# Filling the unused rows of the experts' results inside phase two instead of at the experts' start

## The chip, the cores and the metric

The kernel runs on one core of a Trainium2 chip. The metric is the device time of one execution in microseconds. Three executions of the kernel before took 2258.63, 2264.56 and 2267.71 us; the time that counts is their median, 2264.56 us.

## What is computed

One inference step of one decoder layer, in float32, for a prompt of 2048 tokens and 8 sample tokens with states of their own (D = 1024). What matters here:

```python
h = x + W_out[ concat(mLSTM heads, chunk MLP heads) ]( rmsnorm(x) )
h = h + HierMoE( rmsnorm(h) )        # best group of 4, then top 2 of its 8 SwiGLU experts: 32 experts
h = h + sigmoid(h @ W_pg) * rmsnorm(p @ W_ple)
y = rmsnorm(h)
# an expert's block of 128 rows:
y_block = (silu(xb @ w1[e]) * (xb @ w3[e])) @ w2[e]       # w1, w3: 1024 x 512; w2: 512 x 1024
```

Each token's two results are gathered from the experts' output, weighted and summed. The sample tokens also update a state C (8 x 4 x 128 x 128), which is loaded, changed and stored.

## The kernel before, in words

Tokens are worked in 17 tiles: 16 of 128 prompt tokens (NT = 16, P = 128) and one of the 8 sample tokens. Every matrix product is made from three products of split operands (`w_hi`, `w_lo` and `x_hi`, `x_lo`), so all weights are split after loading: ScalarE makes the high part, VectorE the low part, POOL the low part of the second half of each w1. Four parts of the program follow each other, and each engine's instructions stand in program order; what ties engines together are semaphores.

*Phase one* (until about 560 us) projects q, k, v and the gates and runs the mLSTM.

*Phase two* (about 560 to 1055 us) has the chunk MLP, the out projection, the residual h, the norm hn and the routing. `tiles(step, behind, within)` runs a `step(u, ...)` for each tile on each engine; the tiles named in `behind` and `within` also carry pieces of the sample tokens' work, and only tiles 12 and 13 (of the middle ones) run as a loop on SP. SP's `step` for tile u stores hn of the tile before (`keep_hn`), loads the split x of tile u + 2 (`load_split_x`, once PE has projected with the old one), loads the mLSTM's result (`load_ha`), and when h of this tile is ready (`h_ready`) loads the next residual rows (`load_rows`), stores h (to `h_dram`), and in tile 15 loads half of expert 0's w1 (`load_first`). From tile 3 to 10 VectorE also updates an eighth of the sample state C in each tile (`sample_c`, L1675 to L1683); eighths 2 to 7 are loaded by SP in `load_c` (L1268), right behind the h store. VectorE's order in such a tile: hn of the tile before (`norm_h`, L1548), the chunk MLP's output, the state update (L1679 is the operation that needs the loaded C), the low half of the transposed mix (`mix_rest`, L1567), the routing (L1603 on), gelu and vn (L1572 to L1583), the residual `h_sb` (L1593). PE transposes hn in `hn_transposes` (L241), in the middle of the next projection.

The routing scatters token numbers to `list_dram`, an expert's tokens in a row, and counts. An expert takes as many blocks of 128 rows as its tokens need, at least one.

*The experts* (about 1055 to 1970 us): 32 experts, here 49 blocks in all (at most MAXBLK = 64, since the counts depend on the data). POOL gathers a block's rows of hn by the list (`gather`, L2061) into `rows_in`, after the list entries (L2056), and splits its part of the next expert's w1 behind the blocks of an expert (`split_w1`, L2070). PE transposes the rows of the next block (`transposes`, L2102), multiplies with w1 and w3 (L2113 to L2115) and w2 (L2132 on). ScalarE stores a block's result (`y_dram`, L2170), block i at rows (i + 1) * 128. SP loads weights in the fixed order of `reload(e)`: each half of each matrix as soon as the copy that it overwrites has been split (`wait_lo`). `y_dram` has (MAXBLK + 2) * 128 = 8448 rows, and no row of it may be left unwritten when the last phase's gather takes the whole tensor as its source. So SP, behind the loads for expert 2, reads the number of blocks used (`count_all`) and fills the rest, copying 128 rows of `hn_dram` to each unused block:

```python
total = count_all(sp_)
with sp_.Fori(total + 1, MAXBLK + 2) as i:
    sp_.dma_start(y_dram[bass.ds(i * P, P), :], hn_dram[0:P, :]).then_inc(spare_filled, 16)
with sp_.Fori(0, total) as i:
    sp_.sem_inc(spare_filled, 16)
```

The second loop brings the semaphore to a constant, which SP waits for at the end of the experts. No value of a filled row reaches an output.

*The last phase* (from about 1970 us) gathers the results, adds the per-layer embedding and stores y.

Of the kernel before, what the change touches and what calls it, by code (L numbers as in the profile page):

```python
# [20 lines left out]
P = 128  # L21
# [3 lines left out]
NT = SEQ // P  # L25
# [8 lines left out]
NE = NG * EPG  # L34
FF = 512
KF = FF // P
CAP = SEQ + P
MAXBLK = NE + (SEQ + NS) * 2 // P
PLE = 256
KP = PLE // P  # L40
PARTS = 3
# [38 lines left out]
def program(nc, a, o):  # L80
    with ExitStack() as whole:
        def sem(name):
            return whole.enter_context(nc.semaphore(name))

        def dram(name, shape, dt=F32):
            return nc.dram_tensor(name, shape, dt, kind="Internal").ap()
# [5 lines left out]
        hn_dram = dram("hn_dram", (NTILE * P, D))  # L92
        list_dram = dram("list_dram", (NE * CAP, 1), I32)
        y_dram = dram("y_dram", ((MAXBLK + 2) * P, D))
        xT_dram = dram("xT_dram", (NTILE, 2, P, D))
# [34 lines left out]
        rows_loaded = sem("rows_loaded")  # L130
        entry_loaded = sem("entry_loaded")
        hi_ready = sem("hi_ready")

        def hold(pool, semaphore, value):

            pool.wait_ge(semaphore, value)
            pool.sem_inc(turn, 1)
# [4 lines left out]
        with ExitStack() as body:  # L142
# [3 lines left out]
            with ExitStack() as mix_scope:  # L146
# [40 lines left out]
                x_rows = a["x_prompt"].rearrange("b s d -> (b s) d")  # L187
# [31 lines left out]
                def load_split_x(sp_, u):  # L219

                    for w, dst in enumerate((x_hi, x_lo)):
                        sp_.dma_start(dst[:, :, :].rearrange("p k n -> p (k n)").bitcast(F32),
                                      xT_dram[bass.ds(u, 1), w, :, :].rearrange("a p c -> p (a c)")).then_inc(x2_loaded, 16)
# [862 lines left out]
                with ExitStack() as two_scope:  # L1086
# [107 lines left out]
                    def past(u, n):  # L1194

                        return not isinstance(u, int) or u > n

                    with nc.Block() as block:
                        @block.sync
                        def _(sp_):  # L1200
                            def load_rows(u, r):
                                src = xs_rows if r == NS else x_rows[bass.ds(u * P, P), :]
                                sp_.dma_start(xr_sb[0:r, :], src).then_inc(xr_loaded, 16)

                            def load_ha(u, r):
                                sp_.dma_start(mix[0:r, 0:512], ha_dram[bass.ds(u * P, r), :]).then_inc(ha_loaded, 16)

                            def keep_hn(u, r):
                                sp_.wait_ge(hn_ready, u + 1)
                                sp_.dma_start(hn_dram[bass.ds(u * P, r), :], hn[0:r, :]).then_inc(hn_stored, 16)  # L1210

                            def load_first(c):

                                sp_.dma_start(shared[:, c * RH:(c + 1) * RH].rearrange("p (k n) -> p k n", k=KD // 2),
                                              a["w1"][0, 0, c * D // 2:(c + 1) * D // 2, :].rearrange("(k p) n -> p k n", p=P)).then_inc(raw_loaded[0][c], 16)

                            def step(u, r, r_next, r_last):
                                if past(u, 0):
                                    keep_hn(u - 1, r_last)
                                if r_next == P:  # L1220
                                    sp_.wait_ge(vb_mm, u + 2)
                                    load_split_x(sp_, u + 2)
                                if r_next:
                                    sp_.wait_ge(mix_tp, u + 1)
                                    if r_next == NS:
                                        sp_.wait_ge(d_ha_kept, 16)
                                    load_ha(u + 1, r_next)
                                sp_.wait_ge(h_ready, u + 1)
                                if r_next:
                                    load_rows(u + 1, r_next)  # L1230
                                sp_.dma_start(h_dram[bass.ds(u * P, r), :], h_sb[0:r, :]).then_inc(h_stored, 16)
                                if r_next == NS:
                                    load_first(0)
# [685 lines left out]
            pleg_b = shared[:, 2 * D:3 * D]  # L1919
            p_in = [shared[:, 3 * D + b * PLE:3 * D + (b + 1) * PLE] for b in range(2)]  # L1920
            fing_b = shared[:, 4 * D:5 * D]
            p_rows = a["p_prompt"][0].rearrange("b s d -> (b s) d")
            with ExitStack() as expert_scope:
                def eb(name, shape, dt=F32):
# [18 lines left out]
                parts_of = lambda bank, n: quarter(bank)[:, 0:K_OF[n][1] - K_OF[n][0], :]  # L1943

                (xe_tp, xe_hi_ready, xe_lo_ready, h1_mm, h3_mm, tanh_done, up_done, hid_ready,
                 hid_tp, hidT_hi_ready, hidT_lo_ready, y0_mm, y1_mm, y_in, y_stored, spare_filled, place_steps) = [sem(n) for n in (
                     "xe_tp xe_hi_ready xe_lo_ready h1_mm h3_mm tanh_done up_done hid_ready "
                     "hid_tp hidT_hi_ready hidT_lo_ready y0_mm y1_mm y_in y_stored spare_filled place_steps").split()]

                def span(eng, e):  # L1950

                    first = eng.value_load(blk[0:1, 0, bass.ds(e, 1)], min_val=0, max_val=MAXBLK - 1)
                    end = eng.value_load(blk[0:1, 1, bass.ds(e, 1)], min_val=1, max_val=MAXBLK)
                    return first, end

                def count_all(eng):

                    return eng.value_load(blk[0:1, 1, NE - 1:NE], min_val=1, max_val=MAXBLK)

# [49 lines left out]
                with nc.Block() as block:  # L2009
                    @block.sync  # L2010
                    def _(sp_):
                        def load(e, m, c):

                            kc = (KF if m == 2 else KD) // 2
                            dst = raw[m][:, c * RH:(c + 1) * RH].rearrange("p (k n) -> p k n", k=kc)
                            sp_.dma_start(dst, a[("w1", "w3", "w2")[m]][0, bass.ds(e, 1), c * kc * P:(c + 1) * kc * P, :].rearrange(
                                "a (k p) n -> p (a k) n", p=P)).then_inc(raw_loaded[m][c], 16)

                        def reload(e):

                            for m in range(PARTS):
                                for c in range(2):
                                    wait_lo(sp_, e - 1, m, c)
                                    load(e, m, c)

                        sp_.wait_ge(rows_loaded, 16)
                        for m in (1, 2):
                            for c in range(2):
                                load(0, m, c)
                        reload(1)  # L2030
                        reload(2)
                        total = count_all(sp_)
                        with sp_.Fori(total + 1, MAXBLK + 2) as i:
                            sp_.dma_start(y_dram[bass.ds(i * P, P), :], hn_dram[0:P, :]).then_inc(spare_filled, 16)
                        with sp_.Fori(0, total) as i:
                            sp_.sem_inc(spare_filled, 16)
                        with sp_.Fori(3, NE) as e:
                            reload(e)
                        for n in range(2):
                            for c in range(2):  # L2040
                                wait_lo(sp_, NE - 1, n, c)
                                sp_.dma_start(raw[n][:, c * RH:(c + 1) * RH].rearrange("p (k n) -> p k n", k=KD // 2),
                                              a["w_ple_gate"][0, c * D // 2:(c + 1) * D // 2, n * 512:(n + 1) * 512].rearrange("(k p) n -> p k n", p=P)
                                              ).then_inc(raw_loaded[n][c], 16)
                        wait_lo(sp_, NE, 0, 1)
                        sp_.dma_start(w_ple, a["w_ple"][0].rearrange("(k p) n -> p k n", p=P)).then_inc(late_loaded, 16)
                        sp_.dma_start(pleg_b, a["ple_norm_g"][0, :].partition_broadcast(P)).then_inc(late_loaded, 16)
                        for b in range(2):
                            sp_.dma_start(p_in[b], p_rows[b * P:(b + 1) * P, :]).then_inc(pp_sem[b], 16)
                        sp_.wait_ge(spare_filled, (MAXBLK + 1) * 16)  # L2050

                    @block.gpsimd
                    def _(pool):
# [209 lines left out]
        with ExitStack() as late:  # L2263
# [22 lines left out]
            hz = sb("hz", [P, 544])  # L2286
            pT = [hz[:, b * PLE:(b + 1) * PLE].rearrange("p (k n) -> p k n", k=KP) for b in range(2)]
            st3 = hz[:, 512:544]
# [28 lines left out]
            with nc.Block() as block:  # L2317
# [113 lines left out]
                def _(act):  # L2431
                    def pT_copy(t, b, r, bank=PT):
                        act.wait_ge(ptp, t + 1)
                        src = bank[:, 0:PLE].rearrange("p (k n) -> p k n", k=KP)
                        act.activation(pT[b][:, :, 0:r], src[:, :, 0:r], ACT.Copy).then_inc(pT_ready, 1)
# [109 lines left out]
```

## Time and profile before

| | us |
|---|---|
| median of three runs | 2264.56 |
| their range | 2258.63 to 2267.71 |
| the profiled execution, its own time | 2255.27 |
| its span | 2253.7 |
| PE busy | 2149.3 (95%) |
| VectorE (DVE) busy | 1430.6 (63%) |
| ScalarE (ACT) busy | 971.0 (43%) |
| POOL busy | 581.7 (26%) |

PE, DVE, ACT and POOL are the tensor, vector, scalar and GpSimd engines; SP issues most DMAs. "L2034" is a line of the kernel. In a timeline a row gives the start, the duration and the instruction, with "x4" for merged ones and in brackets how long the engine was idle before it and what ended that. A row of waits reads: engine, tile and line that waited, what it waited for, total us, times, longest us. In a row of a DMA issue "x1, 512.0 KB, 10.9" is the number, the size of one and the median us from issue to landing. PEclk is the clock granted to PE, as a share of the full 2.4 GHz (0.50 is 1.2 GHz).

### The profile page before, as it was taken

To read this page: it belongs to the slowest core of one execution; us is meant where nothing else is said; L and a number is where in the kernel's file an instruction comes from. 1 tells how busy PE (TensorE), PEld (TensorE's weight loads), DVE (VectorE), ACT (ScalarE), POOL (GpSimd) and SP (SyncE) were. 2 spreads that over 40 slices of the span, in tenths; PEclk is the share of its full clock that TensorE was granted. 3 is DMA by queue.
4 is the path that set the end of the run, shared out by engine and by line. 5 is a ranking of instruction groups with operands and counts; after the bars stand their busy time and mean duration, and the time that the engine had idled before them with its cause. 6 is when DMAs were issued, how large, how long until landed. Compare 5 with 4: busy or idle time off the path is not lost. (4 is left out here: it accounts for less than half of the span.)

```text
span 2253.7 us, 34056 instructions
## 1 busy us (share of the span) xinstructions
PE 2149.3 (95%) x10539; PEld 1773.2 (79%) x10540; DVE 1430.6 (63%) x2866; ACT 971.0 (43%) x1569; POOL 581.7 (26%) x595
## 2 busy tenths in 40 slices
PE   6999999999899999994889999999999999899998
PEld 5878888888788888884778888888888878767775
DVE  5788888888566665564536465665566566846554
ACT  4433344444432222222435465665556465623332
POOL 1121111111244333332121223233332132233332
PEclk9999999999999999996999999999999999999999
DMA  6111110132534333324787677898787778943441
GB/s 231 60 38 66 65 60 37 65 112 92 187 107 136 121 121 117 103 91 147 292 309 256 219 266 289 292 363 289 283 294 260 289 290 305 334 169 125 158 141 49
DMA packets 160333, 407.13 MB, mean 181 GB/s; under 512 B 18835, under 2 KB 22347, under 8 KB 160014
## 3 DMA queue, kind: packets, MB, share of 16 engines
q1 hardware_dynamic: 138518, 337.17, 42.0%
q0 software_dynamic: 14560, 43.11, 5.8%
q10 hardware_dynamic: 7200, 26.22, 2.9%
q8 instruction: 23, 0.38, 0.1%
q14 instruction: 32, 0.26, 0.0%
HBM read 330.12 MB, written 84.82 MB: 184 GB/s over the span
## 5 line engine op out<-in xcount | busy, mean ns | idle before, releaser
L234 PE MATMUL bank<-w_hi,mix_x 128*128 128x512 f32 x816 | 333.3, 408 | 9.9 <-DMA mix_x<-xT_dram 4.0
L236 PE MATMUL bank<-w_hi,mix_x 128*128 128x512 f32 x816 | 323.8, 397 | 0.0
L235 PE MATMUL bank<-w_lo,mix_x 128*128 128x512 f32 x816 | 322.9, 396 | 0.0
L2113 PE MATMUL bank<-w_hi,x_hi 128*128 128x512 f32 x784 | 307.6, 392 | 8.1 <-POOL w_lo L2070 4.6
L2212 DVE TENSOR_TENSOR w_lo<-raw,w_hi 128x2048 fp32r<-128x2048 f32 x130 | 292.6, 2311 | 34.8 <-ACT w_hi L2149 34.7
L2115 PE MATMUL bank<-w_hi,x_lo 128*128 128x512 f32 x784 | 307.1, 392 | 0.0
L2114 PE MATMUL bank<-w_lo,x_hi 128*128 128x512 f32 x784 | 307.1, 392 | 0.0
L2149 ACT ACTIVATE w_hi<-raw 128x2048 fp32r<-128x2048 f32 x130 | 238.8, 1925 | 4.8 <-DMA raw<-in_w 4.8
L2070 POOL TENSOR_TENSOR w_lo<-shared,w_hi 128x2048 fp32r<-128x2048 f32 x31 | 157.2, 5071 | 231.7 <-DMA shared<-hn_dram,entry 131.9
L234 PEld LDWEIGHTS bank<-w_hi,mix_x 128*128 128x128 f32 x816 | 156.7, 192 | 42.0 <-issue 5.1
L236 PEld LDWEIGHTS bank<-w_hi,mix_x 128*128 128x128 f32 x816 | 156.3, 192 | 34.7
L235 PEld LDWEIGHTS bank<-w_lo,mix_x 128*128 128x128 f32 x816 | 156.7, 192 | 29.9
L2113 PEld LDWEIGHTS bank<-w_hi,x_hi 128*128 128x128 f32 x784 | 148.5, 189 | 39.9 <-POOL w_lo L2070 5.0
L2115 PEld LDWEIGHTS bank<-w_hi,x_lo 128*128 128x128 f32 x784 | 148.4, 189 | 31.0
L2114 PEld LDWEIGHTS bank<-w_lo,x_hi 128*128 128x128 f32 x784 | 148.5, 189 | 30.9
L248 POOL TENSOR_SCALAR stat<-stat 128x4 f32<-128x4 f32 (+3 forms) x67 | 13.4, 200 | 514.2 <-ACT junk L716 271.2
L2061 POOL DMA_INDIRECT shared<-hn_dram,entry x49 | 68.2, 1392 | 282.9 <-DMA entry<-list_dram 139.3
L2149 ACT ACTIVATE hidT_hi<-bank 128x128 fp32r<-128x128 f32 x98 | 37.6, 384 | 226.3 <-PE bank L2121 226.3
L2217 DVE SCALAR_TENSOR_TENSOR up<-tanh_h,bank 128x512 f32<-128x512 f32 x49 | 33.5, 684 | 157.4 <-ACT tanh_h L2174 157.4
L2132 PE MATMUL bank<-w_hi,hidT_hi 128*128 128x512 f32 x392 | 126.6, 404 | 0.0
L2132 PE MATMUL bank<-w_lo,hidT_hi 128*128 128x512 f32 x392 | 122.3, 393 | 0.0
L2149 ACT ACTIVATE w_hi<-shared 128x2048 fp32r<-128x2048 f32 x64 | 119.7, 1921 | 4.7 <-DMA shared<-in_w 3.9
(316 smaller groups left out, 4222.1 us busy)
## 6 DMA issues: line engine op xcount, KB each, us to landing
raw<-in_w SPq DMA_DIRECT2D x128, 1024.0 KB, 8.5
shared<-in_w SPq DMA_DIRECT2D x64, 1024.0 KB, 8.6
y_dram<-y_sb ACTq DMA_DIRECT2D x50, 512.0 KB, 6.9
xT_dram<-mix_x SPq DMA_DIRECT2D x34, 512.0 KB, 3.5
mix_x<-xT_dram SPq DMA_DIRECT2D x34, 512.0 KB, 4.5
shared<-in_w_in SPq DMA_DIRECT2D x24, 512.0 KB, 6.5
small<-in_x_prompt SPq DMA_DIRECT2D x16, 512.0 KB
xr_sb<-in_x_prompt SPq DMA_DIRECT2D x16, 512.0 KB
```

The source lines that it names most:

```text
L234: pe.matmul(bank[:, :], x_hi[:, k, :], wh[:, k, :], start=(k == 0), stop=False)
L235: pe.matmul(bank[:, :], x_hi[:, k, :], wl[:, k, :], start=False, stop=False)
L236: ins = pe.matmul(bank[:, :], x_lo[:, k, :], wh[:, k, :], start=False, stop=(k == KD - 1))
L2061: pool.indirect_dma_start(out=rows_in[:, :], out_offset=None, in_=hn_dram[0:NT * P + NS, :], in_offset=bass.IndirectOffsetOnAxis(ap=entry[ ...
L2070: pool.tensor_tensor(w_lo[slot(j, 0)][:, cols], raw[0][:, cols], w_hi[slot(j, 0)][:, cols].bitcast(F32), ALU.subtract).then_inc(w1_lo, 1)
L2113: pe.matmul(bank[:, :], x_hi[:, k, :], wh[:, k, :], start=(k == 0), stop=False)
L2114: pe.matmul(bank[:, :], x_hi[:, k, :], wl[:, k, :], start=False, stop=False)
L2115: ins = pe.matmul(bank[:, :], x_lo[:, k, :], wh[:, k, :], start=False, stop=(k == KD - 1))
L2132: pe.matmul(Y[n][:, :], hidT_hi[:, k, :], col(w, k, n), start=(k == 0 and w is wh), stop=False)
L2149: return act.activation(out, in_, ACT.Copy)
L2212: dve.tensor_tensor(w_lo[slot(j, m)][:, cols], raw[m][:, cols], w_hi[slot(j, m)][:, cols].bitcast(F32), ALU.subtract).then_inc(w1_lo if is ...
L2217: STT(up[:, :], tanh_h[:, :], 1.0, H1[:, :], ALU.add, ALU.mult).then_inc(up_done, 1)
```

## The change

The unused rows are no longer found out and filled at the experts' start. Instead, in phase two, SP's step of each of the 16 tiles with 128 tokens copies SPARE = (64 + 1 - 32) * 128 / 16 = 264 rows of the prompt's input `x_rows` to `y_dram`, between `load_rows` and the h store. Together they fill rows 33 * 128 to 8447, that is every block that could be unused with any counts (there are always at least 33 blocks). The blocks among them that are used are overwritten later by their results. SP waits for all 16 copies before it loads the first experts' weights; the value load, both loops and the wait at the end are gone.

```diff
+SPARE = (MAXBLK + 1 - NE) * P // NT
...
+        spare_filled = sem("spare_filled")
...
                                 sp_.wait_ge(h_ready, u + 1)
                                 if r_next:
                                     load_rows(u + 1, r_next)
+                                if r == P:
+                                    sp_.dma_start(y_dram[bass.ds(u * SPARE + (NE + 1) * P, SPARE), :], x_rows[0:SPARE, :]).then_inc(spare_filled, 16)
                                 sp_.dma_start(h_dram[bass.ds(u * P, r), :], h_sb[0:r, :]).then_inc(h_stored, 16)
                                 if r_next == NS:
                                     load_first(0)
...
+                        sp_.wait_ge(spare_filled, 16 * NT)
                         sp_.wait_ge(rows_loaded, 16)
                         for m in (1, 2):
                             for c in range(2):
                                 load(0, m, c)
                         reload(1)
                         reload(2)
-                        total = count_all(sp_)
-                        with sp_.Fori(total + 1, MAXBLK + 2) as i:
-                            sp_.dma_start(y_dram[bass.ds(i * P, P), :], hn_dram[0:P, :]).then_inc(spare_filled, 16)
-                        with sp_.Fori(0, total) as i:
-                            sp_.sem_inc(spare_filled, 16)
                         with sp_.Fori(3, NE) as e:
                             reload(e)
...
-                        sp_.wait_ge(spare_filled, (MAXBLK + 1) * 16)
```

SP's instructions in a tile of phase two that loads a piece of the state, before (`xr_sb`: residual rows; `hn_dram`: store of the norm; `mix_x`: split x; `mix`: mLSTM's result):

```order
L1203 DMA xr_sb<-in_x_prompt 128x1024
L1231 DMA h_dram<-h_sb 128x1024
L1268 DMA shared<-in_state_C 128x512
L1274 DMA out_C_s<-shared 128x512
L1210 DMA hn_dram<-shared 128x1024
L222 DMA mix_x<-xT_dram 128x1024 x2
L1206 DMA mix<-ha_dram 128x512
```

and now:

```order
L1205 DMA xr_sb<-in_x_prompt 128x1024
L1234 DMA y_dram<-in_x_prompt 32x8448
L1235 DMA h_dram<-h_sb 128x1024
L1272 DMA shared<-in_state_C 128x512
L1278 DMA out_C_s<-shared 128x512
L1212 DMA hn_dram<-shared 128x1024
L224 DMA mix_x<-xT_dram 128x1024 x2
L1208 DMA mix<-ha_dram 128x512
```

The copy of 264 rows (as 32 x 8448 elements) stands ahead of the h store, the state's piece and everything else of the tile; the line numbers of what follows it are higher by 2 to 4. 

SP's instructions at the experts' start, before (`raw<-in_w`: w3 and w2, here the last halves of expert 2's; `shared<-in_w`: w1):

```order
L2016 DMA raw<-in_w 128x2x1024 x2
L1958 TENSOR_LOAD blk
L1958 ISA x2
L2033 ISA
L2033 UNCONDITIONAL_BRANCH
L2033 ISA
L2034 DMA y_dram<-hn_dram 16x8192
L2033 REGISTER_ALU
L2033 COMPARE_AND_BRANCH
L2035 UNCONDITIONAL_BRANCH
L2035 REGISTER_ALU
L2035 COMPARE_AND_BRANCH
```

and now:

```order
L2020 DMA raw<-in_w 128x2x1024 x2
L2037 UNCONDITIONAL_BRANCH
L2037 ISA
L2020 ISA
L2020 DMA shared<-in_w 128x4x512
L2020 ISA
```

Behind the loads for expert 2 the value load, the loop of copies (L2033, L2034) and the loop of increments (L2035) are gone, and the loop over the experts from 3 on (before L2037) follows at once.

## Rows read from the trace of the kernel before

**Rows 1.** Stages; columns: us, each engine busy (instructions), PEclk, DMA share, GB/s

```profile
620.00:1020.00 400.00, 397.64 (x2069) 337.62 (x2069) 243.31 (x748) 112.89 (x311) 140.13 (x179) 1.00 0.35 116
1120.00:1140.00 20.00, 17.54 (x83) 14.34 (x81) 3.52 (x7) 3.32 (x7) 1.55 (x2) 1.00 1.03 382
1140.00:1160.00 20.00, 16.18 (x68) 13.71 (x69) 12.10 (x9) 12.88 (x11) 7.27 (x3) 0.83 0.97 359
1260.00:1960.00 700.00, 693.45 (x3255) 571.24 (x3254) 433.36 (x405) 414.14 (x431) 207.96 (x102) 1.00 0.81 295
```

**Rows 2.** Waits of PE, 1060 to 1270

```profile
PE bank L2102 <- DMA shared<-hn_dram,entry: 7.6, 4, 6.3
```

**Rows 3.** Timeline of PE, 1105 to 1184; start us, us, instruction, [idle before <-releaser]

```profile
1105.12 0.79 PE L2113 MATMUL bank<-w_hi,x_hi 128*128 128x512 f32 x1 [4.58 <-POOL w_lo L2070]
...
1120.24 0.60 PE L2102 MATMUL bank<-ident,shared 128*128 128x128 f32 x4
...
1143.82 1.11 PE L2102 MATMUL bank<-ident,shared 128*128 128x128 f32 x4 [6.27 <-DMA shared<-hn_dram,entry]
1144.93 1.06 PE L2102 MATMUL bank<-ident,shared 128*128 128x128 f32 x4
...
1164.91 0.60 PE L2102 MATMUL bank<-ident,shared 128*128 128x128 f32 x4
...
1182.87 0.60 PE L2102 MATMUL bank<-ident,shared 128*128 128x128 f32 x4
```

**Rows 4.** Timeline of SP's queue, 1100 to 1170

```profile
1107.25 6.97 SPq L2016 DMA_DIRECT2D raw<-in_w  x4
1115.42 15.10 SPq L2034 DMA_DIRECT2D y_dram<-hn_dram  x16
1146.20 3.56 SPq L2016 DMA_DIRECT2D shared<-in_w  x2
```

**Rows 5.** Timeline of POOL; then gathers, KB and us to landing, 1128:1129.5 and 1150:1157

```profile
1128.64 0.98 POOL L2061 DMA_INDIRECT shared<-hn_dram,entry  x1 [6.50 <-DMA entry<-list_dram]
...
shared<-hn_dram,entry POOLq DMA_INDIRECT x1, 15.1
...
shared<-hn_dram,entry POOLq DMA_INDIRECT x1, 8.9
```

**Rows 6.** DMA issues 1260:1960; first and last fill; stage 1120 to 1122

```profile
shared<-hn_dram,entry POOLq DMA_INDIRECT x38, 6.0
...
y_dram<-hn_dram SPq DMA_DIRECT2D x1, 512.0 KB, 10.9
...
y_dram<-hn_dram SPq DMA_DIRECT2D x1, 512.0 KB, 22.2
...
1120.00:1122.00 2.00, 2.00 (x16) 1.83 (x15) 0.57 (x2) 1.07 (x3) 0.43 (x1) 1.00 1.04 424
```

**Rows 7.** Timeline of SP's queue in one tile, 822 to 850

```profile
824.74 0.43 SPq L1268 DMA_DIRECT2D shared<-in_state_C  x1
833.12 0.81 SPq L222 DMA_DIRECT2D mix_x<-xT_dram  x2
```

**Rows 8.** The stage from 828 to 830 in that tile

```profile
828.00:830.00 2.00, 2.00 (x15) 1.74 (x14) 1.41 (x3) 0.22 (x1) 1.70 (x2) 1.00 1.04 410
```

**Rows 9.** Waits of DVE in tiles 5 to 10, 703 to 870

```profile
DVE mixT_lo L1567 <- ACT mixT_hi L1426: 14.4, 6, 2.7
DVE shared L1679 <- DMA shared<-in_state_C: 3.6, 6, 0.9
```

**Rows 10.** Timeline of DVE in that tile

```profile
830.24 0.75 DVE L1679 SCALAR_TENSOR_TENSOR shared<-shared 128x512 f32<-128x512 f32 x1 [0.80 <-DMA shared<-in_state_C]
834.71 1.29 DVE L1567 TENSOR_TENSOR mixT_lo<-bank,mixT_hi 128x512 fp32r<-128x512 f32 x2 [2.27 <-ACT mixT_hi L1426]
853.03 1.28 DVE L1548 SCALAR_TENSOR_TENSOR shared<-h_sb,stat,small 128x1024 f32<-128x1024 f32 x1 [0.95 <-POOL stat L251]
```

**Rows 11.** Timeline of PE, transposes of hn

```profile
855.42 1.03 PE L241 MATMUL bank<-ident,shared 128*128 128x128 f32 x8
```

More of the change, by code:

```diff
@@ L1945, in program @@
                 (xe_tp, xe_hi_ready, xe_lo_ready, h1_mm, h3_mm, tanh_done, up_done, hid_ready,
-                 hid_tp, hidT_hi_ready, hidT_lo_ready, y0_mm, y1_mm, y_in, y_stored, spare_filled, place_steps) = [sem(n) for n in (
+                 hid_tp, hidT_hi_ready, hidT_lo_ready, y0_mm, y1_mm, y_in, y_stored, place_steps) = [sem(n) for n in (
                      "xe_tp xe_hi_ready xe_lo_ready h1_mm h3_mm tanh_done up_done hid_ready "
-                     "hid_tp hidT_hi_ready hidT_lo_ready y0_mm y1_mm y_in y_stored spare_filled place_steps").split()]
+                     "hid_tp hidT_hi_ready hidT_lo_ready y0_mm y1_mm y_in y_stored place_steps").split()]
                 def span(eng, e):
```

## The prediction, made before the change was run

> **What bounds the kernel now.** I read the stages first. PE is busy for 397.64 of the 400 us from 620 to 1020 (phase two) and for 693.45 of the 700 us from 1260 to 1960 (the later experts), at a granted clock of 1.00 in both [rows 1]. So whatever does not make PE wait costs nothing, and the reader should look for places where PE waits. From 1120 to 1160 it is busy for only 17.54 and 16.18 us of 20, and in the second row the clock is 0.83 on average, between the levels of 1.2 and 2.4 GHz [rows 1].
>
> Then PE's waits at the start of the experts (1060 to 1270): the first is 7.6 us for the gathered rows in four waits, 6.3 of them in one [rows 2]. PE's timeline places the long one: idle 6.27 us until 1143.82 [rows 3]. The second group of row transposes stands at 1120.24, 1144.93, 1164.91 and 1182.87, and by then a block has its usual length, 17.96 us. The two blocks before took 24.69 and 19.98. Against 17.96 that is 6.73 + 2.02 = **8.8 us** too many: the wait, and matmuls at the lower clock after it. The block before them holds a wait of 4.58 us for POOL's w_lo, until 1105.12, ten microseconds ahead of the first fill, so the change can't take that one away.
>
> Then the queues beside that wait. SP issues the 16 fills from 1115.42 to 1130.5 and gets to the first half of expert 3's w1 only at 1146.20; the 49 semaphore increments of L2035 and L2036 fill the 15.7 us between [rows 4]. POOL issues a gather at 1128.64, in the middle of the fills. It lands 15.1 us later, at 1143.7, 0.1 us before PE starts again [rows 5], where the median of the later 38 is 6.0 [rows 6].
>
> **What goes from the experts' start.** The 16 fills, their queue's backlog and SP's loop all go. The gather, issued at 1128.64 at the latest, lands after 6.0 us, at 1134.6, if it is as fast as the later ones; with the 8.9 us of the one after it [rows 5] it lands at 1137.5. PE asks for it at 1143.82 - 6.27 = 1137.55. Both ends cover it, the second only just; that its list entry also comes through the backlog gives a little more room. What is late next? The w1 half of expert 3, which SP could not issue before 1146.20, can go at 1116; its second half waits for POOL's split of expert 2's w1, which POOL begins when the gather has landed, and so moves forward with it. So no new wait takes the place, and I count the whole 8.8 us. SP's own saving (30.8 us of issuing and counting) is worth nothing more. The other three waits for a gather, 1.3 us together [rows 2], are not counted; with them the gain would be 10.1 us, the upper end.
>
> **What phase two takes on.** Each of the tiles 0 to 15 now copies 264 rows of 4 KB, 1.081 MB from HBM to HBM: 17.3 MB instead of 8.4, because the filled region no longer depends on the counts. It stands on SP's queue behind load_rows and ahead of the h store. No wait is added on SP before the experts, and there only a wait for the 16 fills, the last of which is issued in tile 15, before the routing of the last tiles and the first gather. SP's 0.52 us per issue falls in such gaps as the one before 833.12 [rows 7]. What matters is the 1.081 MB ahead of what comes behind it on the queue. How long is that? Upper bound: of the 16 old fills the first, issued at 1115.4, landed after 10.9 us and the last, issued at 1130.0, after 22.2 [rows 6]: 15 fills of 0.524 MB in 25.9 us, 304 GB/s beside other traffic, so 3.6 us. Lower bound: the queue moved 424 GB/s from 1120 to 1122 [rows 6], so 2.5 us. In phase two nothing but SP's transfers is large and the rate is 410 GB/s from 828 to 830 [rows 8], so I take **2.6 us**, nearest to the lower bound.
>
> Most followers have room. The h store is wanted a tile (some 27 us) later; hn's store, the x halves and ha come behind waits of their own; the x halves go out 8.4 us after the state's piece (833.12 and 824.74 [rows 7]), when the fill is through or nearly so, and are used only once the out projection is through. In tile 15 the fill, the h store and the first half of w1 stack up, but that half is split only after the last tile's routing.
>
> One follower has little room: the state_C load of tiles 5 to 10, issued right behind the h store. VectorE waits for it already, 3.6 us in 6 waits [rows 9]; in the tile of rows 7 it waits 0.80 us, until 830.24 [rows 10]. Behind it on VectorE the state update runs, then mixT_lo, which waits for ScalarE anyway: 14.4 us over these six tiles, 2.4 each [rows 9]. A delay X eats that first. What is left runs down one chain without a gap: routing, gelu, vn, h_sb, and, through ScalarE and POOL, hn (853.03 + 1.28 = 854.31), which PE transposes at 855.42: 1.1 us of room [rows 10, 11]. The chain also issues the next tile's fill, so lateness adds up from tile to tile, and the cost over six tiles is 6X - 14.4 - 1.1 us, if positive. X = 2.5 gives nothing, X = 2.6 gives 0.1, X = 3.6 gives 6.1. I take **0.5 us**, with 0 and 6 as ends.
>
> **Sum.** 8.8 - 0.5 = 8.3 us. The profiled execution took 2255.3 us (span 2253.7), so 2247.0 for it. It is 9.3 us shorter than the median of the three timed runs; I assume that those have the same stall, so the forecast for the median is 2264.6 - 8.3 = **2256.3 us**, 0.37% faster. About 0.5% (11.3 us) is what a measurement of this kernel can tell from no change.
>
> **The rivals.**
> *The stall is not the fills' (2265 us).* If the DMA engines take turns between queues, a gather of 0.5 MB waits only about its own length beside a backlog: at 400 GB/s shared by two, 2.6 us and a few for the way, about 6. Then the 15.1 us come from something else, such as the 4 MB of weights issued from 1107.25 [rows 4], and nothing is won; with the 0.5 us of phase two, 2265. For: the next gather, with weights but no fills issued just ahead, is slow too, 8.9 us [rows 5]. Against: that is far from 15.1. The Trainium skill, "DMA: Bandwidth & Descriptors", section "Queues, rings and completion order", says both that each engine takes the queues in turn packet by packet, and that a completion count lands only after all earlier writes of that engine across queues; the first speaks for this rival, the second against it.
>
> *The timed runs lose more there (2247 us).* They are 9.3 us above the profiled one. A gather that races with 16 fills can come out worse than in this trace. If the 9.3 us lie there, they go too: 17.6 us, 2247. Nothing in the one trace shows where they lie.
>
> *The fill is slow and VectorE's chain becomes the bound of six tiles (2272 us).* This ends on the other side. A fill moves every byte out of HBM and back in. If it gets only half of the 410 GB/s for that, X is 5.3 us, and it costs 6 * 5.3 - 15.5 = 16.3 us: 2264.6 - 8.8 + 16.3 = 2272, PE waiting at its transposes of hn in tiles 6 to 10. The change loses from 6X - 15.5 > 8.8 on, X = 4.05 us or 267 GB/s, which is under the 304 of the upper bound; it is slower by over 0.5% from X = 5.9 on. Against: 382 GB/s over 1120 to 1140, most of it bytes of fills [rows 1]. The Trainium skill, "HBM Reference", section "Specifications (TRN2)", gives about 358 GB/s as a core's share of HBM; if a copy's reads and writes both counted against it, a fill would take an estimated 6.0 us, cost 20.5 us and give 2276. The trace disagrees, as its 382 GB/s of mostly copied bytes is over twice what that allows.
>
> That the change doesn't do what it says has no chance worth a number: the program has the 16 copies in phase two and none behind the weights.
>
> **Chances.** Forecast 0.56; stall stays 0.14; more goes 0.23; slow fill 0.07, of which 0.05 over 0.5% slower. The likeliest gives 2256.3. The range reaches from 2247 (more goes) to 2267 (stall stays, with a few microseconds of phase two), leaving out the slow fill and the tails. Faster by over 0.5%: 0.23. Within 0.5%: 0.56 + 0.14 + 0.02 = 0.72. Slower: 0.05.
>
> **What would show it.** PE's row transposes should stand 18 us apart from the third block on, with no wait over 1 us for the gathered rows and a clock of 1.00 from 1120 on. That gather should land within 6 to 9 us. SP should issue expert 3's first w1 half right behind expert 2's loads. In phase two VectorE's waits for state_C should grow from 3.6 to about 19 us and those of mixT_lo fall from 14.4 to near 0, with PE still busy over 99% from 620 to 1020. The forecast is wrong if the gather still takes over 10 us, if PE shows waits for hn in tiles 6 to 10, or if a fill takes over 4 us.

## The result, and the profile after

| | before | after |
|---|---|---|
| median, us | 2261.6 (4 runs, 2257.83 to 2267.71) | 2276.52 (4 runs, 2275.39 to 2278.7) |
| profiled execution, its span | 2255.27, 2253.7 | 2275.39, 2273.8 |
| six tiles that wait for state_C (5 to 10) | 160.7 | 180.8 |
| tiles 3 and 4 | 53.5 | 57.9 |
| first row transposes of the experts | 1055.88 | 1080.54 |
| the six blocks behind them, to the seventh block's row transposes | 126.99 | 119.32 |

The ratio is 1.0065 [1.0037, 1.0092]: the change makes the kernel 0.65% slower, 15 us, where 8.3 us less was forecast (2256.3 us, with a range from 2247 to 2267). A tile's length is the time from one `load_rows` issue of SP to the next. SP's step u opens tile u + 1: steps 2 and 3 open tiles 3 and 4, steps 4 to 9 tiles 5 to 10.

The experts' start did what was forecast. Waits of PE, 1060 to 1300, in the changed kernel, to be held against [rows 2]:

```profile
PE bank L2101 <- DMA shared<-hn_dram,entry: 2.7, 2, 1.7
```

Timeline of PE there, against [rows 3]:

```profile
1130.19 0.80 PE L2112 MATMUL bank<-w_hi,x_hi 128*128 128x512 f32 x1 [4.60 <-POOL w_lo L2069]
1145.50 0.66 PE L2101 MATMUL bank<-ident,shared 128*128 128x128 f32 x4 [1.68 <-DMA shared<-hn_dram,entry]
1146.11 0.60 PE L2101 MATMUL bank<-ident,shared 128*128 128x128 f32 x4
...
1164.04 0.60 PE L2101 MATMUL bank<-ident,shared 128*128 128x128 f32 x4
...
1181.93 0.60 PE L2101 MATMUL bank<-ident,shared 128*128 128x128 f32 x4
...
1199.86 0.60 PE L2101 MATMUL bank<-ident,shared 128*128 128x128 f32 x4
```

The wait for w_lo is still there, 4.60 us. The group at 1146.11 answers to the one at 1120.24 before. Behind it three blocks take 17.93, 17.89 and 17.93 us, 53.75 together, where they took 24.69 + 19.98 + 17.96 = 62.63. SP's queue and the gather, against [rows 4, 5]; the last row is the DMA issues from 1152 to 1154:

```profile
1125.79 4.75 SPq L2020 DMA_DIRECT2D shared<-in_w  x2
1132.32 6.97 SPq L2020 DMA_DIRECT2D raw<-in_w  x4
1141.31 21.65 SPq L2020 DMA_DIRECT2D shared<-in_w  x2
```

```profile
shared<-hn_dram,entry POOLq DMA_INDIRECT x1, 4.1
```

No fills stand in the queue, and the gather issued at 1153.17 lands after 4.1 us. The 4 MB of weights are issued 20.9 us ahead of it, as they were before (21.4 us), so it was not they that made it late. One wait for rows is longer than was forecast: 1.68 us at 1145.50, where it was 0.57.

Phase two is where the time went. Stages of the changed kernel, with the columns of [rows 1]:

```profile
620.00:1020.00 400.00, 384.68 (x1965) 323.46 (x1964) 225.29 (x697) 106.86 (x292) 131.22 (x169) 0.98 0.48 149
...
1260.00:1960.00 700.00, 692.40 (x3240) 570.75 (x3238) 420.26 (x397) 406.02 (x425) 207.81 (x102) 1.00 0.79 287
```

PE is busy for 384.68 us of 400 instead of 397.64, at 0.98 of its clock. Waits of DVE from 590 to 1060:

```profile
DVE vn L1587 <- POOL stat L260: 54.2, 15, 6.5
DVE mixT_lo L1571 <- ACT mixT_hi L1430: 46.9, 11, 6.4
DVE shared L1683 <- DMA shared<-in_state_C: 40.2, 6, 8.7
```

State_C is now waited for 40.2 us in six waits, where it was 3.6 [rows 9]: each came X = 36.6 / 6 = **6.1 us** later. The waits for ScalarE's mixT_hi, which were the room, are 46.9 where the kernel before had 59.7 in all of phase two; in the six tiles 0.2 us is left of their 14.4, near 0 as was forecast. What went beyond that room reaches PE; its waits from 590 to 1060:

```profile
PE bank L1341 <- DVE idx L1669: 8.4, 5, 2.6
PE bank L1382 <- DVE mixT_lo L1571: 6.9, 4, 2.3
```

Neither row is in the kernel before. One tile shows the way, in DVE's timeline and then PE's, against [rows 10, 11]:

```profile
735.70 0.75 DVE L1683 SCALAR_TENSOR_TENSOR shared<-shared 128x512 f32<-128x512 f32 x1 [8.53 <-DMA shared<-in_state_C]
...
737.81 1.28 DVE L1571 TENSOR_TENSOR mixT_lo<-bank,mixT_hi 128x512 fp32r<-128x512 f32 x2
```

```profile
739.14 3.53 PE L1382 MATMUL bank<-w_hi,mixT_lo 128*128 128x512 f32 x8 [2.00 <-DVE mixT_lo L1571]
```

VectorE stood for 8.53 us, did not wait for mixT_hi afterwards, and still had mixT_lo ready 2.00 us too late. Its queue in SP's timeline, and the landings of the copies and of the state pieces from 620 to 1020:

```profile
721.62 0.33 SPq L1205 DMA_DIRECT2D xr_sb<-in_x_prompt  x1
721.99 0.52 SPq L1234 DMA_DIRECT2D y_dram<-in_x_prompt  x1
722.55 0.58 SPq L1235 DMA_DIRECT2D h_dram<-h_sb  x1
723.17 0.43 SPq L1272 DMA_DIRECT2D shared<-in_state_C  x1
```

```profile
y_dram<-in_x_prompt SPq DMA_DIRECT2D x14, 1056.0 KB, 9.9
...
shared<-in_state_C SPq DMA_DIRECT2D x6, 256.0 KB, 11.1
list_dram<-tok,idx POOLq DMA_INDIRECT x28, 7.8
```

Before, the same state pieces landed after 5.3 us and the small stores of the list after 4.3. The tiles differ: in the six, the copy lands after 10.1, 10.9, 6.9, 9.8, 7.6 and 9.7 us and the state piece after 12.5, 12.6, 8.2, 10.9, 8.4 and 11.4. How fast did the engines move the bytes meanwhile? Stages of two microseconds from the copy's issue to its landing at 732.1, with [rows 8] (410 GB/s) as the rate that the forecast took:

```profile
722.00:724.00 2.00, 2.00 (x13) 1.75 (x12) 0.94 (x10) 1.12 (x3) 0.77 (x2) 1.00 0.70 211
724.00:726.00 2.00, 2.00 (x12) 1.69 (x12) 1.97 (x3) 0.25 (x1) 1.67 (x1) 1.00 1.31 322
726.00:728.00 2.00, 2.00 (x15) 1.74 (x14) 1.16 (x2) 0.50 (x2) 1.69 (x2) 1.00 0.87 253
728.00:730.00 2.00, 2.00 (x11) 1.65 (x10) 0.00 (x0) 0.59 (x2) 0.00 (x0) 1.00 0.75 304
730.00:732.00 2.00, 2.00 (x18) 1.83 (x16) 0.00 (x0) 0.80 (x2) 0.12 (x1) 1.00 1.05 390
```

The mean of the five is 296 GB/s. Single stages are rough: the copy goes in pieces of 33 KB, and a DMA share of 1.31, more than there is, says that their bytes are not booked evenly.

A second piece was in no part of the forecast: tiles 3 and 4 take 29.7 and 28.2 us instead of 26.8 and 26.7, before any of the late state pieces is needed. POOL's timeline and DVE's in tile 3:

```profile
681.57 0.72 POOL L1802 TENSOR_SCALAR tok<-tok 128x1 int32<-128x1 int32 x1 [4.64 <-DMA list_dram<-tok,idx]
...
690.79 0.25 POOL L260 TENSOR_SCALAR stat<-stat 128x4 f32<-128x4 f32 x1 [0.20 <-POOL stat L253]
```

```profile
691.08 1.14 DVE L1587 SCALAR_TENSOR_TENSOR vn<-ge,stat,small 128x128 f32<-128x128 f32 x4 [6.53 <-POOL stat L260]
```

POOL waits until its store of the list has landed before it steps the token numbers (1.38 us before, 4.64 now), then does the sample tokens' norm, which in this tile fills the time until VectorE wants the statistics of vn. So VectorE waits 6.53 us, where the longest such wait was 3.5.

The balance of the two profiled executions: 24.66 us lost until the first transposes, 7.67 us won in the first six blocks, 3.4 us given back in the later blocks (from the seventh block's transposes to ScalarE's last store of a block 783.9 us before, 787.3 after): 20.4, beside the spans' 20.1. Of the 24.66, 20.1 lie in tiles 5 to 10 and 4.4 in tiles 3 and 4.

### The profile page after: what moved, and what is told of

Same layout as the page of the kernel before. It is cut to its first block and busy times, and to the rows that moved or that the text cites. A ratio compares the mean times of both kernels' runs of the same rounds, so it can differ in the third digit from the quotient of the medians.

```text
span 2273.8 us, 33844 instructions
## 1 busy us (share of the span) xinstructions
PE 2158.3 (95%) x10539; PEld 1777.4 (78%) x10540; DVE 1427.6 (63%) x2866; ACT 970.5 (43%) x1569; POOL 579.6 (25%) x595
## 2 busy tenths in 40 slices
DMA packets 160589, 416.05 MB, mean 183 GB/s; under 512 B 18835, under 2 KB 22347, under 8 KB 160014
## 5 line engine op out<-in xcount | busy, mean ns | idle before, releaser
L2113 PEld LDWEIGHTS bank<-w_lo,x_hi 128*128 128x128 f32 x784 | 148.3, 189 | 30.9
```

Of the source, the lines that this page charges most:

```text
L2113: pe.matmul(bank[:, :], x_hi[:, k, :], wl[:, k, :], start=False, stop=False)
```

## Experiments

Two theories for the six tiles: the **order of the queue** (the state piece stands behind 1 MB on SP's queue), and the **bytes beside it** (a copy on any queue slows the piece). A third, that the **size of the pieces** of the copy makes it slow. For each kernel X is taken from VectorE's waits for state_C, less 3.6, over six.

**The fill behind the state pieces.**

```diff
 def step(u, r, r_next, r_last):
     if past(u, 0):
+        sp_.dma_start(<fill of tile u - 1>).then_inc(spare_filled, 16)
         keep_hn(u - 1, r_last)
...
-    if r == P:
-        sp_.dma_start(<fill of tile u>).then_inc(spare_filled, 16)
     sp_.dma_start(h_dram[bass.ds(u * P, r), :], h_sb[0:r, :]).then_inc(h_stored, 16)
```

> The 16 copies of 264 rows stay in phase two and on SP's queue; only their place in a tile moves, from ahead of the h store to behind the state's load and store. Theory Q (order in the queue: the copy stands ahead of the state_C load, for which VectorE waits): the load lands after 5 to 6 us again, VectorE's wait for state_C over tiles 5 to 10 falls from 40.2 us to under 8, the six tiles lose their 20 us, and the kernel takes about 2276.5 - 20 = 2256 us. Theory B (bytes: a copy inside HBM slows every transfer beside it, wherever it is issued): hn's store, split x and ha suffer instead, the tiles stay some 4 us too long, 2270 to 2277 us. Theory S (the large pieces of 33 KB take long on single DMA engines): the load is free of them, as under Q, but the scatters of POOL still land late (7.7 us median instead of 4.3).

Measured: 2256.43 us (10 runs), ratio 0.9983 [0.9971, 0.9995]. Waits of DVE and of POOL, 590 to 1060:

```profile
DVE shared L1682 <- DMA shared<-in_state_C: 5.3, 6, 1.4
```

```profile
POOL tok L1801 <- DMA list_dram<-tok,idx: 17.1, 6, 8.0
```

Moving the copy a few places down the same queue, with every byte still moved, gives back all of the six tiles (26.8 each). Tiles 3 and 4 keep 29.7 and 28.2, and POOL still waits: their loss is another one.

**The fill where the queue is idle**, right behind the load of the next mLSTM rows and ahead of the wait for h.

```diff
         load_ha(u + 1, r_next)
+        sp_.dma_start(<fill of tile u>).then_inc(spare_filled, 16)
     sp_.wait_ge(h_ready, u + 1)
...
-    if r == P:
-        sp_.dma_start(<fill of tile u>).then_inc(spare_filled, 16)
```

> The copy is issued behind the load of ha, 17 us ahead of the next h store, where the queue of the kernel before is empty (0 GB/s). Theory Q: all 24 us of phase two come back, and the gain at the experts' start stays: 2276.5 - 24 = 2252 to 2256 us, the fastest of the three; VectorE's wait for state_C at 3 to 4 us. Theory B: the copy has the DMA engines to itself there, so also little loss, 2252 to 2260. If it stays at 2270 or more, the cost is not in phase two's transfers at all, but in what the removed fills did for the experts.

Measured: 2251.1 us (4 runs), ratio 0.9952 [0.9934, 0.9969], and once more in more rounds:

> The same kernel as with the fill in the idle place, in more rounds: 2251, the kernel before 2261; ratio 0.995 to 0.996. If the first comparison was luck, the ratio is 0.998 or more.

2252.34 us (12 runs), ratio 0.9966 [0.9953, 0.9979]. The first comparison was on the kind side; together they say 8 to 10 us faster than the kernel before; by the ratios (0.9966 and 1.0065) that is some 22 us faster than the change. All tiles from 3 to 10 are back at 26.6 to 27.0 us. Landings of the copy from 620 to 1020 in the first of the two, and the stages of one copy:

```profile
y_dram<-in_x_prompt SPq DMA_DIRECT2D x15, 1056.0 KB, 7.3
```

```profile
836.00:838.00 2.00, 2.00 (x13) 1.77 (x13) 1.93 (x6) 0.61 (x3) 1.80 (x2) 1.00 0.98 393
838.00:840.00 2.00, 2.00 (x10) 1.64 (x9) 1.75 (x8) 0.00 (x0) 0.61 (x2) 1.00 1.25 481
840.00:842.00 2.00, 2.00 (x11) 1.65 (x10) 1.67 (x10) 0.20 (x1) 0.00 (x0) 1.00 0.63 270
```

The same instruction with the same bytes lands in 7.3 us here (7.0 to 7.4 in the six tiles) and in 9.9 in the change's place (6.9 to 10.9), and the engines move 381 GB/s in the mean of these three stages, not 296. It is not that fewer bytes stand ahead of it: here the split x and ha, 1.31 MB, are issued just ahead, in the change's place 0.52 MB. But nothing is issued behind it on SP's queue for 16 us, where the change has 1.05 MB.

**The fill on ScalarE's queue**, behind its square of h.

```diff
-    if r == P:
-        sp_.dma_start(<fill of tile u>).then_inc(spare_filled, 16)
...
+    if r == P:
+        act.dma_start(<fill of tile u>).then_inc(spare_filled, 16)
```

> The copies are issued at the same time as in the change, right after h is ready, but from ScalarE's queue, so nothing on SP's queue stands behind them in order. Theory Q: the state load no longer waits for a place behind 1.08 MB: its landing falls from 8 to 12.6 us to about 6 to 7, VectorE's wait for it from 40.2 us to 10 or less, time 2256 to 2262. Theory B: the same bytes run at the same time and share the same engines, so the state load still lands after 8 us or more, VectorE still waits 25 us or more, time 2266 to 2277.

Measured: 2267.61 us (7 runs), ratio 1.003 [1.0013, 1.0046]. DVE's waits and landings in phase two:

```profile
DVE shared L1683 <- DMA shared<-in_state_C: 24.3, 6, 4.6
```

```profile
shared<-in_state_C SPq DMA_DIRECT2D x6, 256.0 KB, 8.6
```

No copy stands ahead of the state piece in its own queue, and still it comes 3.45 us later (X from 24.3). So the bytes beside it are part of the 6.1, and the order of the queue the rest, though how much that is varies from execution to execution (the change's own placement gave 6.1 and, in a run below, 4.6). It is neither theory alone. The six tiles take 170.6 us.

**The fill in smaller pieces**, in the change's place.

```diff
+    pieces = lambda x: x.rearrange("r (h n) -> (r h) n", h=2).rearrange("(j i) n -> i j n", i=16)
-    sp_.dma_start(<destination>, <source>)
+    sp_.dma_start(pieces(<destination>), pieces(<source>))
```

> Same place, same bytes as the change, but the copy goes in 528 pieces of 2 KB, 33 for each of 16, instead of 32 pieces of 33 KB. Theory S: the copy lands in 4 to 5 us instead of 9.9, the state load in 8 at most, VectorE's wait for it falls below 20 us, time 2262 to 2268. Theories Q and B: the size of a piece changes nothing, 2275 to 2278 us, or worse if the small pieces are slower.

Measured: 2276.07 us (4 runs), ratio 1.0075 [1.0056, 1.0094], with waits of 43.0 us for state_C and a landing of 9.7. The profile counts 528 packets of 2 KB for each copy, where the change has 32 of 33 KB (168525 packets in all instead of 160589). That changes nothing; this theory falls.

**Half the bytes in each place.** `SPARE // 2` rows behind the load of ha, `SPARE // 2` in the change's place, and the wait before the experts for 32 fills instead of 16.

```diff
+        sp_.dma_start(<first 132 rows of tile u's fill>).then_inc(spare_filled, 16)
     sp_.wait_ge(h_ready, u + 1)
...
     if r == P:
-        sp_.dma_start(<all 264 rows>).then_inc(spare_filled, 16)
+        sp_.dma_start(<the other 132 rows>).then_inc(spare_filled, 16)
```

> Each fill of 264 rows is cut into two of 132: one goes out in the queue's idle place, right behind the load of ha and ahead of the wait for h, the other stays in the change's place, ahead of the h store and state_C. If the loss goes by the room that VectorE's chain has (a delay of state_C costs nothing up to about 2.5 us a tile, and all of what lies above), half the bytes delay state_C by about 3.1 us instead of 6.1: VectorE's waits for state_C about 3.6 + 18 = 22 us, the six state tiles 26.8 to 28 us long each, some 4 us lost in all, so about 2255 to 2259 for the median. If every byte in that place costs the same, half of the loss stays: the state tiles 10 us longer in all, 2264.

Measured: 2253.51 us (5 runs), ratio 0.9972 [0.9953, 0.9991]. DVE's waits:

```profile
DVE mixT_lo L1572 <- ACT mixT_hi L1431: 47.6, 13, 6.4
...
DVE shared L1684 <- DMA shared<-in_state_C: 16.1, 6, 3.5
```

This is the plainest picture of room that is used up: state_C is waited for 12.5 us more than before, mixT_hi 12.1 us less, and the six tiles take 160.7 us, as before. Half the bytes gave X = 2.1, a third of the whole's 6.1 (and under half of the 4.6 of the next run), and cost the six tiles nothing. Tile 3 still takes 28.95.

**The fill in the change's place in chosen tiles.** This kernel had `if isinstance(u, int)` to choose them.

```diff
+        if not isinstance(u, int):
+            sp_.dma_start(<fill of tile u>).then_inc(spare_filled, 16)
     sp_.wait_ge(h_ready, u + 1)
...
-    if r == P:
+    if r == P and isinstance(u, int):
         sp_.dma_start(<fill of tile u>).then_inc(spare_filled, 16)
```

> The fill stands in the change's place only in tiles 0, 1, 5 to 10 and 15; in tiles 2 to 4 and 11 to 14 it stands in the idle place. If the 4.3 us lost in tiles 2 and 3 come from the fill beside POOL's small stores of the lists of tokens there (the place behind the state transfers showed the same 29.7 and 28.2 us in those tiles), tiles 2 and 3 are 26.8 to 27.2 us now, and the state tiles keep all of their loss: 180 us for six, waits for state_C about 40 us. Time 2272. If the two are one effect, a lateness that builds up from the first tiles, the state tiles get shorter too, and the time falls under 2268.

Measured: 2273.59 us (4 runs), ratio 1.0066 [1.0043, 1.0088], tiles 3 and 4 at 29.3 and 28.2 us. The experiment missed its aim: on SP only tiles 12 and 13 run as a loop, so the condition chose all the others, and the kernel is the change itself but for two tiles. It says nothing about its question, only that the change's time repeats. It also shows how far one profiled execution can be trusted. In the six tiles this kernel is the change, and yet:

```profile
DVE shared L1685 <- DMA shared<-in_state_C: 31.4, 6, 7.7
```

X is 4.6 here, not 6.1, the six tiles take 174.6 us, not 180.8, and the copy lands after 8.0 us, not 9.9 (medians from 620 to 1020). So a difference of 1.5 us in X, or of 6 us over the six tiles, between two profiles shows nothing by itself.

With the tiles named by number instead, it was made twice:

```diff
+        if not isinstance(u, int) or not 4 <= u <= 9:
...
+    if r == P and isinstance(u, int) and 4 <= u <= 9:
```

> The fill stands in the change's place only in the six steps that also load a piece of state_C (u = 4 to 9), and in the idle place in the ten others. If the two losses of phase two are separate, the six tiles keep theirs (about 180 us instead of 160.8, VectorE waits 35 to 40 us for state_C) and the two tiles ahead of them are back at 26.8 us each, so phase two is 20 us longer than in the kernel before instead of 24.4. The experts' start keeps its gain. Time 2272. If lateness from tiles 2 and 3 carries into the six, they get shorter as well, under 176 us.

Measured: 2268.71 us (10 runs), ratio 1.0041 [1.0022, 1.006]. Tiles 3 and 4 take 26.7 each, tiles 5 to 10 178.2. Waits of DVE:

```profile
DVE vn L1589 <- POOL stat L260: 51.1, 15, 3.5
...
DVE shared L1685 <- DMA shared<-in_state_C: 34.2, 6, 7.8
```

The second kernel has `u in (2, 3)` in the place of `4 <= u <= 9`:

> The fill stands in the change's place only in steps 2 and 3, in which POOL waits for its stores of the lists of tokens and then works out the sample tokens' norm, and in the idle place in the 14 others. If the 4.3 us are made there, the intervals of those two steps are 29 to 30 and 28 us instead of 26.9 and 26.8, the six state tiles are 26.8 each, and the time is 2256 (2252 and 4.3). If they need the state tiles' traffic to be felt, all tiles are 26.8 and the time is 2252.

Measured: 2255.36 us (10 runs), ratio 0.9982 [0.9969, 0.9995]. Tiles 3 and 4 take 30.9 and 29.3, the six behind them 26.8 each. Waits of DVE and POOL:

```profile
DVE vn L1589 <- POOL stat L260: 55.4, 15, 7.7
...
DVE shared L1685 <- DMA shared<-in_state_C: 3.8, 6, 0.8
```

```profile
POOL tok L1804 <- DMA list_dram<-tok,idx: 11.9, 2, 6.3
```

The two losses come apart: copies in steps 4 to 9 make only the long waits for state_C, copies in steps 2 and 3 only the late vn. In the two profiled executions the parts are 17.5 and 6.7 us, 24.2 together, beside 24.5 in the change; that they add up so closely is luck, as the run before shows. Neither needs the other.

**The experts' start: the counting moved.** The kernel before, with SP's loop of semaphore increments behind the loads of all experts; the 16 fills stay.

```diff
-with sp_.Fori(0, total) as i:
-    sp_.sem_inc(spare_filled, 16)
 with sp_.Fori(3, NE) as e:
     reload(e)
+with sp_.Fori(0, total) as i:
+    sp_.sem_inc(spare_filled, 16)
```

> The kernel before, with the 16 fills where they were, behind the first experts' weights, and SP's loop of 33 semaphore increments put behind the loads of all the experts. SP then reaches the first half of expert 3's w1 about 8 to 10 us earlier. If PE's stall at the third group of row transposes is the fills' alone (the gather lands late because of their bytes), nothing changes: the wait of some 6 us stays, 2261, ratio 0.999 to 1.001. If SP's lateness with the weights carries the stall or what follows, the time falls by 3 us or more, ratio under 0.9985.

(The loop has 49 turns, one for each block used, not 33.) Measured: 2269.89 us (10 runs), ratio 1.0034 [1.0023, 1.0045]: 9 us slower, which neither had. At the experts' start, SP's queue, the gather of that stretch, and PE:

```profile
1118.05 15.11 SPq L2034 DMA_DIRECT2D y_dram<-hn_dram  x16
1133.66 21.98 SPq L2016 DMA_DIRECT2D shared<-in_w  x2
```

```profile
shared<-hn_dram,entry POOLq DMA_INDIRECT x1, 15.3
```

```profile
1124.82 1.11 PE L2102 MATMUL bank<-ident,shared 128*128 128x128 f32 x4 [3.07 <-DMA shared<-hn_dram,entry]
...
1150.04 1.12 PE L2102 MATMUL bank<-ident,shared 128*128 128x128 f32 x4 [4.46 <-DMA shared<-hn_dram,entry]
```

SP now issues the weights right behind the fills, and the gather, issued at 1134.72, is as late as before, 15.3 us. PE waits 3.07 + 4.46 us for rows. So the late gather goes with the fills, not with the place of the counting; the first half of the expectation holds. What the move costs shows at the other end:

```profile
1961.93 0.93 SPq L2042 DMA_DIRECT2D shared<-in_w_ple_gate  x2
```

```profile
1977.12 0.47 PE L2121 MATMUL bank<-ident,hid 128*128 128x128 f32 x1 [8.43 <-DVE hid L2222]
```

SP issues the last expert's weights until 1946.57 and the last phase's first weights only at 1961.93, 15.4 us later, where the kernel before leaves 1.8 us between them (1936.45 and 1938.29): the counting stands there now. The split of those weights on VectorE, which comes ahead of the last block's `hid`, waits for them, and PE 8.43 us for that. A loop that was free behind expert 2's loads is not free at the end of the queue. The two profiled executions differ by 18.2 us, twice the medians' 9; where the rest lies was not followed up.

Not tried: the change without any fill at all, which would have given the floor, since rows that the last gather's source covers would then never have been written.

## Why the prediction was wrong

**What goes from the experts' start: right.** 8.8 us was counted for the three blocks behind the second group of transposes; they take 62.63 - 53.75 = 8.88 us less. That the w_lo wait stays and that the w1 half follows expert 2's loads at once both came true. Around it 1.2 us are lost in the blocks ahead, where the waits for rows grew from 1.04 to 2.69 us, and 3.4 in the later ones, where they are 7.7 us from 1180 on, against 6.4 from 1160 before. These were not in the forecast; with the fill in other places the waits from 1180 on were 6.7, 7.9 and 11.2, so they vary from execution to execution.

**"So I take 2.6 us, nearest to the lower bound": the step that failed.** The delay of the state piece, X, was 6.1 (4.6 in a second profile of the same placement), so the cost that was put at 0.5 us was 20.1. The formula built on X held roughly: 6X - 15.5 gives, and the six tiles lost,

| kernel | X | 6X - 15.5 | measured |
|---|---|---|---|
| the change | 6.1 | 21.1 | 20.1 |
| smaller pieces | 6.6 | 23.9 | 24.1 |
| change's place in steps 4 to 9 | 5.1 | 15.1 | 17.5 |
| change's place in all but tiles 12 and 13 | 4.6 | 12.3 | 13.9 |
| ScalarE's queue | 3.45 | 5.2 | 9.9 |
| half the bytes | 2.1 | 0 | 0.0 |
| behind the state pieces | 0.3 | 0 | 0.0 |

It falls short by 4.7 us on ScalarE's queue, and no run tells why (the copy's issue stands on ScalarE itself there, which makes mixT_hi), and elsewhere by 2.4 us at most. So the room of 15.5 us, read from the waits for mixT_hi and the 1.1 us to PE, was right in size, and X was mis-sized. Both ends of it (2.5 and 3.6) divided the copy's bytes alone by a rate seen elsewhere. The 2.6 that was taken used a rate at which loads and stores of SBUF ran ([rows 8], 410 GB/s); with the copy among them five stages gave 296 GB/s, by which 1.081 MB are 3.7 us. The rest, up to 4.6 or 6.1, stays open. A likely part, not isolated here, is that the piece also shares the engines with all that stands around it, as the run on ScalarE's queue shows for the bytes beside it.

The sentence of the Trainium skill, "HBM Reference", section "Specifications (TRN2)", of about 358 GB/s for a core, gave X = 6.0 and 2276 us, and 2276.5 was measured. The agreement is not its mechanism's. In the idle place the three stages moved 2.29 MB in 6 us, 1.08 MB of them the copy's; with these counted twice, read and written, that is an estimated 560 GB/s, which a limit of 358 on reads and writes together would not allow. And the 2276 lacks the 4.4 us of tiles 3 and 4 and starts from a median that is 3 us too high (2264.6, against 2261.6 beside the change). The number was right by luck and the reason wrong.

**"Most followers have room": half right.** It named only what follows on SP's own queue. POOL's small store of the list is on another queue, and its landing went from 4.3 to 7.8 us. In tile 3, where POOL works out the sample norm behind that wait, this reached VectorE and then PE: 4.4 us, shown by the run with steps 2 and 3 alone (6.7 there).

**Where PE would wait: right chain, another place.** It was said to be the transposes of hn in tiles 6 to 10. PE waits for mixT_lo itself (L1382), and at the chunk MLP (L1341), which needs vn of its tile and `idx` of an earlier one, so the end of VectorE's work on a tile. The 1.1 us that the forecast added behind hn stood for a path that was not the first to run out; PE's wait for hn is 0.8 us before and after.

**The rivals.** The slow fill, with a chance of 0.07, was what happened: a late state piece makes VectorE's chain the bound of six tiles. Its X of 5.3 lies between the two that were measured. That its time (2272) came near is partly luck, since it knew nothing of tiles 3 and 4, and its reason, a fill at half of the rate because every byte goes out and back in, is not shown: the same copy is through sooner in the idle place. The stall was the fills': with them gone and the weights still there the gather lands after 4.1 us, and with the fills kept and the counting moved it takes 15.3. Weights do delay a gather, as the rival said, but less: one issued among them at 1136.41, with no fills left, takes 9.0 us. That the timed runs lose more than the trace of before is partly so: its later blocks (from ScalarE's fifth store to the last) took 805.3 us, the shortest of eleven profiled executions (the kernel with the counting last apart); the ten others took 806.0 to 813.7, with 808.2 in their middle. So some 3 us of the 6.3 between the execution profiled before and its median may lie there. This is not shown, since the ten others are other kernels, and nothing in one profile could show it. Where the others lie is open.

**What a better version looks like.** The idea of the change was sound and its place was not: in the idle place it gains 8.5 us by the larger comparison (ratio 0.9966), about the 8.3 that was forecast for it, since there the fill really is hidden.

## What to carry to other kernels

A large copy that "fits in the gaps" must be placed against the queue, not against the engines: look for the load behind it that someone waits for, and put the copy where the next instruction on its queue is a long wait for something else. Size a delay by the rate of a stage with the same kind of traffic, and where none exists let the range reach to half of the rate that you have. Then ask of each small transfer on other queues who waits for its landing, in the very tile where that engine has the most to do.

## What was unexpected of the hardware

- One and the same 1.081 MB copy from HBM to HBM landed after 7.3 us with 1.31 MB issued just ahead of it and nothing behind it on its queue, 7.7 on ScalarE's queue, and, with 0.52 MB issued just ahead of it and 1.05 MB behind, 9.9 in one profile and 8.0 in another. While it ran the engines moved 381 GB/s in the first case and 296 in the last.
- A transfer on another queue delays small ones by several microseconds: state pieces of 256 KB from 5.3 to 8.6 us, scatters of 128 numbers from 4.3 to 7.8 (medians; the copy on ScalarE's queue and on SP's).
- Twice the bytes was more than twice the delay: 0.54 MB gave 2.1 us, 1.081 MB 4.6 and 6.1.
- Pieces of 33 KB or of 2 KB made no difference to a copy, 9.9 and 9.7 us.
